# Keeping the one-hot matrices of an expert index in memory between two quarters of a product-key layer

## The reference, cut to what matters

```
q = (x @ w_q).reshape(b, s, 8, 2, 128)
sc = einsum('bshcd,hcnd->bshcn', q, sub_keys)          # 8 heads, 2 halves, 128 keys
s1, i1 = top_k(sc[..., 0, :], 16);  s2, i2 = top_k(sc[..., 1, :], 16)
cand = s1[..., :, None] + s2[..., None, :];  cidx = i1[..., :, None] * 128 + i2[..., None, :]
top_s, pos = top_k(cand, 16);  eidx = take_along_axis(cidx, pos);  gate = softmax(top_s)
hid = gelu(einsum('btd,bthkd->bthk', x, u[eidx]))
out = einsum('bthk,bthkd->btd', gate * hid, v[eidx])
```

## Time and profile before

| what | value |
| --- | --- |
| median of three runs | 2067.51 us (2065.72 to 2070.63) |
| the profiled execution | 2066.06 us, of this the span 2064.3 us |
| granted TensorE clock, mean | 0.999 of full speed |
| TensorE (PE) busy | 2022.8 us, 98% |
| VectorE (DVE) busy | 1377.7 us, 67% |
| ScalarE (ACT) busy | 1004.1 us, 49% |
| GpSimd (POOL) busy | 818.1 us, 40% |
| line 832, the narrow spreads | 2048 matrix multiplies |
| line 841, the wide spreads | 1024 matrix multiplies |
| line 1808, the making of B | 128 instructions of 1217 ns |

### The profile page before, as it was taken

One profiled execution on the slowest core, in us unless ns is written; L12 is line 12 of the kernel. 1 busy time (PEld: TensorE's weight loads), 2 busy tenths in 40 slices (PEclk: granted clock), 3 DMA queues, 4 the chain that ended last, 5 costly groups with the idle time before them and its releaser, 6 DMA issues.

```text
span 2064.3 us, 41422 instructions
## 1 busy us (share of the span) xinstructions
PE 2022.8 (98%) x15380; PEld 1783.0 (86%) x15386; DVE 1377.7 (67%) x2853; ACT 1004.1 (49%) x1533; POOL 818.1 (40%) x358
## 2 busy tenths in 40 slices
PE   7999999999999999999999999999999999999999
PEld 7989999788888888888899899988888888888888
DVE  6573899987666766444465739989876676655443
ACT  6574444334444444444566644433444444444444
POOL 5536720004434343444555477100134344444444
PEclk9999999999999999999999999999999999999999
DMA  7414443444555454555453144434454555455553
GB/s 268 146 33 184 160 154 128 163 163 178 181 177 181 180 182 182 185 195 190 165 187 140 44 162 164 143 125 162 163 183 183 183 184 183 176 183 190 183 186 119
DMA packets 49229, 342.64 MB, mean 166 GB/s; under 512 B 5856, under 2 KB 7008, under 8 KB 7904
## 3 DMA queue, kind: packets, MB, share of 16 engines
q1 hardware_dynamic: 48688, 337.94, 45.2%
q10 hardware_dynamic: 432, 3.21, 0.4%
HBM read 340.08 MB, written 1.05 MB: 165 GB/s over the span
## 4 chain that ended last, share of the span: by engine, by line
PE 88%; DVE 6%; ACT 3%; issue 2%; POOL 1%; DMA 0%; DVEq 0%; SPq 0%; POOLq 0%; ACTq 0%
PE psum L476 18%; PE psum L478 17%; PE psum L867 17%; PE psum L477 17%; PE psum L869 8%; PE psum L832 2%; PE psum L841 1%; POOL wl L383 1%; PE psum L727 1%; ACT wh L371 1%; DVE wl L383 1%; PE psum L802 1%; PE psum L592 1%; PE psum L741 1%; PE psum L742 1%
## 5 line engine op out<-in xcount | busy, mean ns | idle before, releaser
L383 POOL TENSOR_TENSOR wl<-ring,wh 128x1024 fp32r<-128x1024 f32 x336 | 795.1, 2387 | 1207.6 <-ACT wh L371 1207.6
L371 ACT ACTIVATE wh<-ring 128x1024 fp32r<-128x1024 f32 x628 | 643.6, 1047 | 317.2 <-PE psum L478 310.2
L867 PE MATMUL psum<-xx,wh 128*128 128x512 f32 x1504 | 534.1, 398 | 0.0
L869 PE MATMUL psum<-xx,wl 128*128 128x256 f32 x1504 | 418.5, 278 | 0.0
L476 PE MATMUL psum<-wh,Wh 128*128 128x512 f32 (+1 forms) x1056 | 412.7, 391 | 2.8 <-DVE Wl L1856 1.8
L478 PE MATMUL psum<-wh,Wl 128*128 128x512 f32 (+1 forms) x1056 | 408.3, 387 | 0.0
L477 PE MATMUL psum<-wl,Wh 128*128 128x512 f32 (+1 forms) x1056 | 407.8, 386 | 0.0
L383 DVE TENSOR_TENSOR wl<-ring,wh 128x1024 fp32r<-128x1024 f32 x292 | 343.7, 1218 | 62.9 <-ACT wh L371 62.9
L867 PEld LDWEIGHTS psum<-xx,wh 128*128 128x128 f32 x1504 | 282.4, 188 | 63.5
L869 PEld LDWEIGHTS psum<-xx,wl 128*128 128x128 f32 x1504 | 283.1, 188 | 1.1
L476 PEld LDWEIGHTS psum<-wh,Wh 128*128 128x128 f32 x1056 | 198.3, 188 | 46.3 <-issue 5.4
(11 more groups left out here) (265 smaller groups left out, 2728.5 us busy)
## 6 DMA issues: line engine op xcount, KB each, us to landing
ring<-stream SPq DMA_DIRECT2D x318, 1024.0 KB, 4.8
arena<-keys ACTq DMA_DIRECT2D x2, 1024.0 KB, 6.7
smr<-rows SPq DMA_DIRECT2D x1, 1090.0 KB, 14.2
smr<-rows ACTq DMA_DIRECT2D x1, 1090.0 KB, 5.2
h<-x SPq DMA_DIRECT2D x2, 512.0 KB, 6.5
out<-h SPq DMA_DIRECT2D x3, 256.0 KB, 2.1
sm<-cols SPq DMA_DIRECT2D x1, 704.0 KB, 10.2
kst<-consts SPq DMA_DIRECT2D x1, 431.5 KB, 8.8
```

Source lines behind the costliest of these rows:

```text
L371: nc.scalar.activation(wh[:, buffer_of(L, n), c], ring[:, (L * SLOTS + n) % RING, c], ACT.Copy).then_inc(hi_ok, 1)
L383: eng.tensor_tensor(wl[:, b, c], ring[:, (L * SLOTS + n) % RING, c], wh[:, b, c].bitcast(F32), ALU.subtract).then_inc(done, 1)
L867: pe.matmul(bank(4 + e, 512), w[0][:, e, k, :], xx[:, k, :, :].rearrange("p a t -> p (a t)"), start=(k == 0), stop=False, skip_group_check ...
L869: ins = pe.matmul(bank(4 + e, SEQ), w[1][:, e, k, :], xh[:, k, :], start=False, stop=(k == DC - 1), skip_group_check=True)
```

## The change

It has six parts.

1. In the first phase B has three buffers instead of two: the two halves of Bh and the area of GL, which is free until the gelu of pair 16.
2. SyncE stores each of the 16 B matrices of the first quarter to a DRAM tensor `kept` (512 KB each, `keep`). VectorE waits for the store of block n - 3 before it writes B of block n.
3. In the rounds of the first quarter VectorE makes no B. SyncE fetches it (`fetch`), blocks 1 and 0 after the last spread of the first phase, and each later one when the spread of two blocks earlier is done. The ring's loads and these transfers stand in one list, which is no longer a loop.
4. The spread of the second quarter becomes `spread_kept`: it waits for the fetched B and for the added pieces of the block before, and then does `spread_wide` (16 matrix multiplies with 64 columns). VectorE gets `pieces_added` for it, at the end of the next round.
5. ScalarE copies the gates out between the two halves of its high parts, one round later in its own list.
6. The conversion of the two indices to bfloat16 (one VectorE instruction, line 1783) is done by ScalarE, which signals `idx_ok`.

```
+        B_first = (Bh[:, 0], ar(A_GL, TB * P // 2).bitcast(F16).rearrange("p (b c) -> p b c", b=TB), Bh[:, 1])
+        kept = nc.dram_tensor("kept", (LAYERS, NB, P, TB * P), F16).ap()
...
+            def keep(L, n):
+                sp.wait_ge(b_ok, (QUARTERS - 1) * NB * L + n + 1)
+                sp.dma_start(kept[L, n], B_first[n % 3].rearrange("p b c -> p (b c)")).then_inc(kept_st[n % 3], 16)
+            def fetch(L, n):
+                if n < 2:
+                    for j in range(3):
+                        sp.wait_ge(kept_st[j], 16 * (L + 1) * KEPT[j])
+                sp.wait_ge(g_ps, (L * QUARTERS + 1) * NB + (n - 1 if n >= 2 else -n))
+                sp.dma_start(Bh[:, n % 2].rearrange("p b c -> p (b c)"), kept[L, n]).then_inc(kept_ld[n % 2], 16)
+            KEEP_AT = {u_slot(p): min(x + 2, NB - 1) for x, p in AFTER.items()}
...
+                while n in KEEP_AT and done <= KEEP_AT[n]:
+                    keep(L, done)
+                    done += 1
+                if n == u_slot(QP):
+                    fetch(L, 1)
+                    fetch(L, 0)
                 sp.wait_ge(slot_used, k - RING + 1)
                 sp.dma_start(ring[:, k % RING, :], stream[k]).then_inc(slot_ld[k % RING], 16)
+                if n in V_ALL[0:NB - 2]:
+                    fetch(L, V_ALL.index(n) + 2)
...
+                def spread_kept(i, k):
+                    pe.wait_ge(kept_ld[k % 2], 16 * (NB // 2 * L + 2 * i + k // 2 + 1))
+                    if isinstance(i, int) and 4 * i + k == 0:
+                        pe.wait_ge(g_ok, q0 + NB)
+                    else:
+                        pe.wait_ge(gm_ok, (QUARTERS - 1) * NB * L + 4 * i + k)
+                    spread_wide(q0 + NB + 4 * i + k, k % 2)
...
                         weighted(i, k, 4)
-                        spread(q0 + NB + 4 * i + k, k % 2)
+                        spread_kept(i, k)
...
+                act.wait_ge(rout_ps, L + 1)
+                act.activation(idx2[:, :, :, :], last(bank(6, 2, SEQ), 2), ACT.Copy).then_inc(idx_ok, 1)
...
-                        high(L, v_slot(k + 1), i)
-                        gates_out(1, i, k, 4)
+                        high_half(L, v_slot(k + 1), i, 0)
+                        if not isinstance(i, int) or 4 * i + k:
+                            gates_out(1, i, k - 1, 4)
+                        high_half(L, v_slot(k + 1), i, 1)
...
-                step(dve.tensor_copy(idx2[:, :, :, :], last(bank(6, 2, SEQ), 2)))
...
+                    if quarter != 1:
+                        if quarter == 0 and n >= 3:
+                            dve.wait_ge(kept_st[n % 3], 16 * (L * KEPT[n % 3] + n // 3))
+                        dve.tensor_tensor(cut(Bh[:, n % 2, :, :] if quarter else B_first[n % 3]), pairs(idx2[:, 1, at, :], P // 2),
+                                          mid(iota[:, :, :], 1, TB), ALU.is_equal).then_inc(b_ok, 1)
...
                         if not isinstance(i, int) or 4 * i + k < QP - 1:
                             low(i, k + 1)
+                        if not isinstance(i, int) or 4 * i + k:
+                            pieces_added(1, i, k - 1, 4)
```

More of the change, by code:

```diff
@@ L187 @@
 WIDTH[IN_SLOT[I_REM]] = DC * REM
+KEPT = [len(range(j, NB, 3)) for j in range(3)]
 V_STEP = {v_slot(p): 4 if p < QP else 2 for p in range(PAIRS)}
@@ L343, in trunk @@
         gm_ok, hc_ok, hs_ok = sem("gm_ok"), sem("hc_ok"), sem("hs_ok")
+        kept_st, kept_ld = [sem(f"kept_st{j}") for j in range(3)], [sem(f"kept_ld{j}") for j in range(2)]
         gelu_ok, w_ok, acc_ps = sem("gelu_ok"), sem("w_ok"), sem("acc_ps")
@@ L439, in _ @@
             sp.dma_start(ring[:, 3, :], stream[3]).then_inc(slot_ld[3], 16)
[L440 to L445, removed]
+            def keep(L, n):
[8 more added lines that the diff above has]
+            KEEP_AT = {u_slot(p): min(x + 2, NB - 1) for x, p in AFTER.items()}
+            done = 0
+            for k in range(RING, LAYERS * SLOTS):
+                L, n = (k - RING) // SLOTS, (k - RING) % SLOTS
+                if n == 0:
+                    done = 0
+                while n in KEEP_AT and done <= KEEP_AT[n]:
[4 more added lines that the diff above has]
+                    fetch(L, 0)
                 sp.wait_ge(slot_used, k - RING + 1)
                 sp.dma_start(ring[:, k % RING, :], stream[k]).then_inc(slot_ld[k % RING], 16)
+                if n in V_ALL[0:NB - 2]:
+                    fetch(L, V_ALL.index(n) + 2)
             rows_out = out.rearrange("o (t p) d -> p (o t) d", p=P)
@@ L910, in _ @@
                 for n in range(NB):
-                    spread(q0 + n, n % 2, n)
+                    spread(n)
                     if n in AFTER:
@@ L914, in _ @@
                 hidden(0, QP)
-                with pe.Fori(0, QP // 4) as i:
+                for k in range(4):
+                    weighted(0, k, 4)
+                    spread_kept(0, k)
+                with pe.Fori(1, QP // 4) as i:
                     for k in range(4):
                         weighted(i, k, 4)
-                        spread(q0 + NB + 4 * i + k, k % 2)
+                        spread_kept(i, k)
                 hidden_wide(0, LEAD)
@@ L1222, in gates_out @@
                     act.activation(buf[:, :, bass.ds((step * i + n) * TB, TB)],
-                                   (bank(6 + n % 2, TB, QI).rearrange("p t e -> p e t") if quarter < 2 else both_pieces()[:, 0]),
+                                   (bank(6 + n % 2, TB, QI).rearrange("p t e -> p e t") if quarter == 0 else both_pieces()[:, 0]),
                                    ACT.Copy, scale=1.0 / G_SCALE).then_inc(g_ok, 1)
@@ L1907, in _ @@
                 first_quarter(QP // 4 - 1)
-                dve.wait_ge(g_ok, (L * QUARTERS + 2) * NB)
+                pieces_added(1, 0, QP - 1)
+                dve.wait_ge(gm_ok, ((QUARTERS - 1) * L + 1) * NB)
                 weigh(0, QP)
```

48 lines of the change are left out of this document (28 added, 20 removed).

## The result

| | kernel before | changed kernel |
|---|---|---|
| median of 10 runs each | 2068.32 us | 2062.16 us |
| lowest to highest | 2065.72 to 2073.35 | 2058.90 to 2066.99 |
| profiled execution: own time, span, granted clock | 2066.06, 2064.3, 0.999 | 2066.99, 2065.2, 0.994 |

The changed kernel is faster by a ratio of 0.9967, 95% interval [0.9956, 0.9978]: 6.2 us (measured with the two side by side) where 15.0 were forecast. The time stands 0.16 us above the top of the range, which comes from rival 2; but the rounds are not what rival 2 said, as the rows show.

The account below looks back on a forecast made before the run. TensorE was taken to bound the kernel, with VectorE close behind. Per layer 7.0 + 0.5 - 0.7 + 0.7 = 7.5 us, 15.0 over both layers, gave 2051.1 profiled and 2052.5 as median; range 2047 to 2062.

Parts of the forecast that it names:

- rival 2: First quarter's rounds: VectorE becomes the bound at 6.3 us a round, with the full stall at the end; 2060.9 us, chance 0.19.
- the 0.84 and 0.61 waits: TensorE's waits for VectorE at the first phase's start (0.84 us) and before the second `weighted` (0.61 us); both forecast to go.
- the 1.57 waits: TensorE's two later waits for VectorE in the first phase, 1.57 us each; forecast to stay whatever the number of B buffers.
- B of block 3: First phase: VectorE's B that waits for the first store; forecast held about 1.5 us, nearly all hidden from TensorE.
- The end of the rounds: Last round: added pieces behind VectorE's A stalled by GpSimd; loss taken as 0.7 us per layer, bounds 0 and 2.1.
- The first store: First phase: store behind a ring load lands near 303.5; 0.3 us taken off, bounds 0 and 5.1.
- the 1.0 of the conversion: Start of first phase: indices converted by ScalarE, VectorE starts earlier, TensorE's waits of 0.84 and 0.18 go; 1.0 us gained.
- First phase: Conversion gain of 1.0 us less 0.3 for the late store; 0.7 us gained per layer.
- The rounds: First quarter: TensorE and VectorE locked, rounds alternating at 6.115 us on average instead of 6.54; 7.0 us gained per layer.
- The wide spread: First quarter's rounds: spread takes TensorE 0.48 us instead of 0.97; at the sixteenth spread this brings 0.5 more.
- The fetches: First quarter's rounds: fetched B put at 7 us to landing, hidden within 11.6 us; rate 245 GB/s where 160 move before.
- The range: Whole kernel: measured time expected within 2047 to 2062 us, around a forecast of 2050 to 2056 with chance 0.50.

Follow-up runs that it names:

- e3_pieces_first: Changed kernel with the added pieces of block 14 ahead of the next quarter's one-hots in VectorE's last round; 2056.02 us, ratio to before 0.9940.
- e2_store_early: Changed kernel with the stores of blocks 0 and 1 issued ahead of the ring load that waits for a buffer; 2057.48 us, ratio to before 0.9950.
- e13_vector_idx: Changed kernel with the conversion of the indices moved back from ScalarE to VectorE; 2060.78 us, ratio to before 0.9952.
- e5_weigh_first: e3_pieces_first plus, in every round, VectorE's weighing of the next block ahead of E and A and added pieces between low halves; 2055.81 us, ratio to before 0.9930.

## Why the prediction was wrong

- **Direction and mechanism**: right; what failed are sizes, each in a term of the sum. TensorE bounds, the gain comes from the rounds, the fetches are hidden, the 0.84 and 0.61 waits go, the 1.57 waits stay, B of block 3 is held.
- **The end of the rounds ("I take 0.7")**: this step failed. The row of before showed one stall, and I took the value near to it though the upper bound described just what follows from the order: two As behind a running GpSimd. It cost 8.14 - 6.12 = 2.0 a layer, 1.3 more than the sum had; e3_pieces_first gives back all of it. The stall was charged to A alone; in e3_pieces_first E and B, which also read two SBUF tensors, stall in A's place.
- **The first store ("I let it land near 303.5 ... I take 0.3 off")**: failed. B of block 3 could start only at 306.5. I had let the store overlap the load in front of it; the row fits the sum of both. TensorE lost 1.65 in layer 0 and 1.44 in layer 1 where 0.3 stood in the sum, and e2_store_early gives back 1.55 a layer. With it went the 1.0 of the conversion: e13_vector_idx shows that it is worth nothing as long as the store decides. First phase: 1.0 - 1.65 = -0.65 (layer 1: -0.4) instead of +0.7, the largest miss together with the stall and the rounds.
- **The rounds ("so the rounds alternate ... 6.115 on average")**: that TensorE and VectorE hold each other up was right (e5_weigh_first undoes it), its size and the even alternation were not: 6.207, half of it because VectorE's chain is 5.97 and not 5.87. 14 x 0.09 = 1.3 a layer.
- **The wide spread ("0.97 - 0.48 = 0.5")**: it was 0.35; 0.15 of the 0.97 was a hidden wait for VectorE, so VectorE was no longer only "close behind" in the kernel before. TensorE alone came out at 6.05 all the same. The gain of the rounds is thus 0.35 of spread and 0.15 of lock undone, not 0.49 of spread.
- **Sum by rows**: rounds 98.68 - 95.04 = 3.64, last spread 0.35, first phase -0.65: 3.3 in layer 0 and, from the same rows there, 3.6 in layer 1, 6.9 us. At full clock 8.3 is measured, 1.4 more than these stretches explain. In the two profiled executions 0.8 of it lies in the attention part of layer 1: from the wait at 1042.64 to that at 1101.99 before is 59.35 us, the same stretch in the changed kernel 1102.16 - 1043.62 = 58.54. That the change causes this is not shown.
- **The fetches**: hidden, as forecast (median 5.6 us to landing, 6.9 at most). The rate given beside them was off: 1.5 MB in 6.1 us is 258 GB/s by the count that gives 160 before, not 245; nothing rests on it.
- **The clock**: the sum had no term for it. It started from a profile at 0.999 and added 1.45 us for the median. What the change adds is under 1 us by the means, but each short wait that it makes or leaves can cost as much again in a slow stretch.
- **The range**: these terms were each taken near their favourable ends, and came near the unfavourable one (stall 2.0 of 2.1) or between (store 1.65 of 5.1). Rival 2's 2060.9 is nearest to the time, but its reason, rounds of 6.3, did not come true.

## What to carry to other kernels

When an instruction that the bounding engine waits for is put on a busy queue, price all that stands ahead of it at its worst row, the stalls beside another engine above all, and then move it ahead of that: the order, not the amount of work, cost 6.8 us at full clock here (e5_weigh_first). A storing DMA that is to free a buffer belongs ahead of the loads that wait for buffers of their own. Where TensorE has short waits that can't be removed, a few dummy multiplies in them pay if the granted clock shows slow stretches behind them.

## What the runs showed of the hardware

- At a wait of TensorE of 1.2 to 2.6 us, in some executions and not in others, a stretch of about 3.4 us at 1.2 GHz began (310.1 to 313.5 in the rows above), which cost 1.5 us. The Trainium skill (TensorE: Matmul & The Clock Gate, Part 1) has half speed as the resting level, from which activity releases the engine; the trace agrees in the level and in what came before. Why the same wait leads to a slow stretch in one execution and not in the next stays open.
- VectorE's instructions with two SBUF inputs waited out instructions of GpSimd: two As of 0.38 each took 2.60 and 2.63 beside halves of 2.77, E 1.74, B 3.42.
- A wait can hide at the end of a row: a spread of 0.97 was 0.81 of work. The kernel without the other engine's work in the way showed it, and so do two spreads back to back (1.77 less 0.96).
